# Gate blocks signalled column by column, squares between key blocks, and four value pages in the space of the prompt's keys

## The chip, the cores and the metric

One core of one Trainium2 chip runs the whole program in one launch. The metric is the device time of a launch in microseconds (us); less is better. TensorE (PE) multiplies matrices, VectorE (DVE), ScalarE (ACT) and GpSimd (POOL) work on tiles in on-chip memory (SBUF and the PSUM banks that PE writes), and SyncE (SP) issues the DMAs that bring weights and cache pages from HBM.

## What is computed

One inference step of one decoder layer, for a prompt of 512 tokens and a sample group of 8 single tokens (together T = 520 columns). The layer has a head group with stick-breaking attention, an S5 state-space group, cross-attention into 256 memory tokens and a convolutional feed-forward part. The change touches the stretch in which three things run side by side: the S5 gate, the memory keys, and the samples' attention over their cached value pages.

```python
# S5 group: y is 512 channels wide
y = jax.nn.gelu(y.reshape(bsz, t, SSM_WIDTH))
out = y * jax.nn.sigmoid(y @ w_glu + b_glu)            # the gate
...
mix = jnp.concatenate([_rmsnorm(o_sb, g_sb_out), _rmsnorm(o_ssm, g_ssm_out)], axis=-1)
x = x + mix @ w_out
...
m = _rmsnorm(mem, g_mem_kv)                            # memory keys and values
mk = (m @ w_mk).reshape(b, MEM_TOKENS, MEM_HEADS, MEM_HEAD_DIM)
...
k_past = cache_sb_k[l][page_table]                     # 8 samples x 2 pages of 128 tokens
v_past = cache_sb_v[l][page_table]
```

## The kernel before, in words

Everything is held channel-major: a tile has 128 channels on the partitions and tokens along the free axis. Matrices of weights come in 126 blocks of 512 KB, numbered in the order of use. Each block n takes the same path: SP loads it into `w_raw` slot n % 4 (`load_block`, L467 to L470, after the low parts of block n-4 are done); ACT copies its high part to `w_hi` slot n % 2 (`high`, L1238 to L1246, after PE has finished block n-2); POOL subtracts to get the low part `w_lo` in two halves (`low`, L581 to L587; DVE does it for a few early blocks); PE multiplies hi by hi, lo by hi and hi by lo (`three`, L620 to L627), in fp32r. Results of a block go to one of two PSUM slots (`slot(e)`, banks 0 and 1, or 2 and 3 of `pj`), and a slot is free again when DVE has read it: DVE adds to the semaphore `evacuated` with each read, PE adds to `block_done` with each finished block.

Every engine has its program written out by hand, and each runs it strictly in order; semaphores tie them together.

The stretch of the change, on PE (from L1012 on), is: `memory_keys(0)`, `memory_keys(1)`, `gate_columns(0)`, `memory_keys(2)`, `gate_columns(1)`, `memory_keys(3)`, `memory_keys(4)`, `decode_values(0)` and `(1)`, `memory_keys(5)`, the column sums of the squares of gated y (`feature_sums`, L683), `decode_values(2)`, `memory_keys(6)`, `decode_values(3)`, `memory_keys(7)`, and eight small matmuls (L1061), after which the memory values (blocks 26 to 33) begin. A memory-key block is 24 matmuls of 256 columns. A gate block (numbers 18 and 20) is two column blocks of 24 matmuls of 260 columns, one for each PSUM slot. The slots in order are e = 16, 17 (keys), 18, 19 (gate), 20 (keys), 21, 22 (gate), 23 to 27 (keys), so `memory_keys(2)` needs the slot of the first gate column block, and `memory_keys(3)` that of the third.

A gate column block is finished by ACT, which takes the sigmoid in PSUM (`gates`, L1442 to L1446), and by DVE, which multiplies it with y (`gate_y`, L1898 to L1901). In between on ACT stand the high parts of the weights and the squares of the gated y (`square`, L1252), which DVE adds up (`add_square`, L1584 for the first, L1587 for the others); the sum over channels and its inverse root (L1256, L1257) scale y. ACT's functions come in table sets: a change of set is a row of its own (ACT_TABLE_LOAD).

The samples' value pages: 16 pages of 256 KB, multiplied in four groups of four (`decode_values(g)`, L944 to L952, matmuls of 32 columns of weights; it adds 1 to `dav_pg`). Groups 0 and 2 use the buffer `vpg`, groups 1 and 3 `kpg`. SP's queue (L528 to L544) loads groups 0 and 1 early, then waits for `dav_pg` 1 before group 2 and for `dav_pg` 2 before group 3:

```python
            for n in range(22, 26):
                load_block(n)
            eng.wait_ge(dav_pg, 1)
            for m in range(8, 12):
                load_values(m)
            load_block(26)
            load_block(27)
            eng.wait_ge(dav_pg, 2)
            for m in range(12, 16):
                load_values(m)
            load_blocks(28, 40)
```

The prompt's keys `kT` (128 x 2080) are read last by the prompt's scores (`scores`, L885 to L903, which count `qk_done`) and by the store of the keys to HBM (counted by `kv_stored`). After the memory values the same space holds other things.

Of the kernel before, what the change touches and what calls it, by code (L numbers as in the profile page):

```python
# [19 lines left out]
ACT = mybir.ActivationFunctionType  # L20
# [7 lines left out]
T = TP + NS  # L28
# [3 lines left out]
SBW = 512  # L32
AT = SBW // P
HEADS = 8
# [22 lines left out]
MK_SLOT, GLU_SLOT = (16, 17, 20, 23, 24, 25, 26, 27), (18, 19, 21, 22)  # L57
# [44 lines left out]
def build(nc, xT, memT, wblk, cols_d, bc_d, dskip_d, consts_d, pages_d, kpool, vpool, kmem, vmem,  # L102
# [5 lines left out]
    def sem(name):  # L108
        return ctx.enter_context(nc.semaphore(name))
# [4 lines left out]
    with ctx:  # L114
# [28 lines left out]
        kT = sbuf(sbctx, "kT", [P, AT, T])  # L143
# [41 lines left out]
        yT = cube(near, 5632, AT, T)  # L185
# [6 lines left out]
        kpg = sbuf(midctx, "kpg", [P, 4, SBW])  # L192
        vpg = sbuf(midctx, "vpg", [P, 4, SBW])
# [13 lines left out]
        xctx.close()  # L207


        cache_tail = [t[:, :, :].rearrange("p a t -> p (a t)")[:, 4 * LANE * NS:4 * LANE * NS + D] for t in (qT, kT)]  # L210
        qz = [t[:, :, :].rearrange("p a t -> p (a t)")[:, 0:4 * LANE * NS].rearrange(
            "p (f c) -> p f c", f=4) for t in (qT, kT)]
# [29 lines left out]
        kv_stored = sem("kv_stored")  # L242
# [4 lines left out]
        block_done = sem("block_done")  # L247
        evacuated = sem("evacuated")
# [50 lines left out]
        qk_done = sem("qk_done")  # L299
# [25 lines left out]
        dav_pg = sem("dav_pg")  # L325
        dav_read = sem("dav_read")
        m_scaled = sem("m_scaled")
        m_hi_done = sem("m_hi_done")
        m_split = sem("m_split")
        sig_done = sem("sig_done")  # L330
        mix_scaled = sem("mix_scaled")
        s_done = sem("s_done")
# [29 lines left out]
        def col(name, i=0, n=1):  # L362
            return cols[:, COL[name] + i:COL[name] + i + n]
# [8 lines left out]
        def slot(e):  # L372
            return pj[:, 2 * (e % 2):2 * (e % 2) + 2, 0:HALF]
# [73 lines left out]
            return (kpg if n % 8 < 4 else vpg)[:, n % 4, :]  # L447

        def value_slot(m):
            return (vpg if m // 4 % 2 == 0 else kpg)[:, m % 4, :]  # L450

        o_bank = aux[:, 3, :]

# [10 lines left out]
        def _(sp_eng):  # L464
            eng = sp_eng
# [53 lines left out]
            def load_values(m):  # L519
                n = page_of(m)  # L520
                load_page(n, value_slot(m), vpool, vpg_loaded[m % 8])
# [6 lines left out]
            eng.wait_ge(dscore_pg, NS * PAGES)  # L528
            for m in range(8):
                load_values(m)  # L530
            for n in range(22, 26):
                load_block(n)
            eng.wait_ge(dav_pg, 1)
            for m in range(8, 12):
                load_values(m)
            load_block(26)
            load_block(27)
            eng.wait_ge(dav_pg, 2)
            for m in range(12, 16):
                load_values(m)  # L540
            load_blocks(28, 40)
            load_block(40)
            load_block(41)
# [76 lines left out]
        def _(pe):  # L620
# [400 lines left out]
            def gate_columns(g):  # L1021
                n = GLU_AT[g]
                wait_low(pe, n, 1)
                for j in range(2):
                    e = GLU_SLOT[2 * g + j]
                    pe.wait_ge(evacuated, e - 1)
                    for kt in range(AT):
                        if g + j == 0:
                            pe.wait_ge(y_split, kt + 1)
                        if (j, kt) == (0, 2):  # L1030
                            second_half(n)
                        hi, lo = (w[:, j * P:(j + 1) * P] for w in weight(n, kt, 2 * P))
                        ins = three([(slot(e)[:, a, :], hi, lo, halves(h_hi[:, AT + kt, :])[:, a, :],
                                      halves(h_lo[:, AT + kt, :])[:, a, :]) for a in range(2)],
                                    kt == 0, kt == AT - 1)
                ins.then_inc(block_done, 1)

            pe.wait_ge(a_exp, HEADS)
            memory_keys(0)
# [25 lines left out]
            for pair in range(4):  # L1065
                pe.wait_ge(evacuated, N_MV + (1, 2, 4, 6)[pair])
                for part in range(2):
                    n = N_MV + 2 * pair + part
# [168 lines left out]
        def _(act):  # L1237
            order = Order(act, act_order)  # L1238

            def high(n, i=0, step=4):  # L1240
                act.wait_ge(raw_loaded[n % 4], raw_count(n, i, step))
                if n == N_END - 2:
                    act.wait_ge(a_split, FT)
                elif n >= 2:
                    act.wait_ge(block_done, min(n, N_END - 2) - 1 + i * step)
                nc.scalar.activation(w_pair(n)[0], w_raw[:, n % 4, :], ACT.Copy).then_inc(hi_done, 1)  # L1246

            def square(src, width, j, i=0, per=0):

                if not (isinstance(j, int) and j == 0):  # L1250
                    act.wait_ge(acc_added, j + i * per)
                nc.scalar.activation(sq[:, 0:width], src, ACT.Square).then_inc(sq_ready, 1)  # L1252
# [186 lines left out]
                    high(18)  # L1439
            high(19)  # L1440

            def gates(first, last):  # L1442
                for m in range(first, last):
                    act.wait_ge(block_done, GLU_AT[m // 2] + 1)
                    nc.scalar.activation(slot(GLU_SLOT[m]), slot(GLU_SLOT[m]), ACT.Sigmoid,
                                         bias=col("b_glu", m)).then_inc(sig_done, 1)  # L1446

            high(20)
            gates(0, 2)
            high(21)  # L1450
            high(22)
            gates(2, 4)
            nc.scalar.preload_act_table_set("natural_log_exp_and_others")
            act.wait_ge(da_arg, 1)
            act.wait_ge(az_cleared, 1)
            nc.scalar.activation(az[:, :, :, :].rearrange("p t b w -> p (t b) w")[:, :, 8:16],
                                 dz[:, 2, :].rearrange("p (c h) -> p c h", h=HEADS), ACT.Exp).then_inc(da_ready, 1)
            high(23)
            act.wait_ge(evacuated, GLU_SLOT[3] + 1)
            square(yT[:, 0, :], T, 4)  # L1460
            square(yT[:, 1, :], T, 5)
            high(24)
            square(yT[:, 2, :], T, 6)
            square(yT[:, 3, :], T, 7)
            root(2, halves(rinv[:, :]), sums23, SBW)
            high(25)
            high(26)
# [74 lines left out]
            for i in range(FT // 2):  # L1542
                for c in range(2):
                    n = N_GU + 2 * c
# [29 lines left out]
        def _(dve):  # L1574
# [3 lines left out]
            def add_square(j, first, width=T, group=0, i=0, per=0):  # L1578

                dve.wait_ge(sq_ready, j + 1 + i * per)  # L1580
                if first:
                    if group:
                        dve.wait_ge(stats_done, group - 1)
                    nc.vector.tensor_copy(acc[:, 0:width], sq[:, 0:width]).then_inc(acc_added, 1)  # L1584
                else:
                    dve.wait_ge(acc_added, j + i * per)
                    tt(acc[:, 0:width], acc[:, 0:width], sq[:, 0:width], ALU.add).then_inc(acc_added, 1)  # L1587
# [300 lines left out]
            def read_keys(m):  # L1888
                dve.wait_ge(block_done, MK_AT[m] + 1)
                nc.vector.tensor_copy(mkT[:, m, :], slot(MK_SLOT[m])[:, 0, 0:MT]).then_inc(evacuated, 1)  # L1890
# [7 lines left out]
            def gate_y(first, last):  # L1898
                for m in range(first, last):
                    dve.wait_ge(sig_done, m + 1)  # L1900
                    tt(halves(yT[:, m, :]), slot(GLU_SLOT[m]), halves(yT[:, m, :]), ALU.mult).then_inc(evacuated, 1)  # L1901
# [57 lines left out]
            read_keys(1)  # L1959
            split_y(2, 4)  # L1960
            gate_y(0, 2)
            read_keys(2)
            gate_y(2, 4)
            read_keys(3)
            add_square(4, True, T, 2)
            add_square(5, False, T, 2)
            read_keys(4)
            add_square(6, False, T, 2)
            add_square(7, False, T, 2)
            read_keys(5)  # L1970
            inverted(2)
# [265 lines left out]
```

## Time and profile before

| | us |
|---|---|
| median of 3 runs | 928.23 |
| lowest and highest | 927.63, 929.48 |
| the profiled execution's own time | 930.51 |
| its span, first to last instruction | 928.7 |
| PE busy | 868.4 (94%) |
| DVE, ACT, POOL busy | 464.5, 334.1, 310.0 |

The profile is one execution. A row of the timeline gives the start, the length, the engine and line, output and inputs, a count, and in brackets how long the engine had been idle before it and what ended the wait. The granted clock (PEclk) is TensorE's, as a share of full speed. A matmul's length includes the time in which its result drains, so back-to-back matmuls overlap; what counts is the distance between starts.

### The profile page before, as it was taken

To read this page: it belongs to the slowest core of one execution; us is meant where nothing else is said; L and a number is where in the kernel's file an instruction comes from. 1 tells how busy PE (TensorE), PEld (TensorE's weight loads), DVE (VectorE), ACT (ScalarE), POOL (GpSimd) and SP (SyncE) were. 2 spreads that over 40 slices of the span, in tenths; PEclk is the share of its full clock that TensorE was granted. 3 is DMA by queue.
4 is the path that set the end of the run, shared out by engine and by line. 5 is a ranking of instruction groups with operands and counts; after the bars stand their busy time and mean duration, and the time that the engine had idled before them with its cause. 6 is when DMAs were issued, how large, how long until landed. Compare 5 with 4: busy or idle time off the path is not lost.

```text
span 928.7 us, 17749 instructions
## 1 busy us (share of the span) xinstructions
PE 868.4 (94%) x7422; PEld 811.5 (87%) x7422; DVE 464.5 (50%) x660; ACT 334.1 (36%) x491; POOL 310.0 (33%) x241
## 2 busy tenths in 40 slices
PE   5999897989977899899899999999999999999996
PEld 5989896867776889799559989999999999999996
DVE  5979777666513743511233465555566666201013
ACT  6553314443733432321332443333333333322231
POOL 4100002000144665344003534444444444445450
PEclk9999998987989999999999999999999999999999
DMA  8221203233325348521841223222232322232322
GB/s 308 70 70 46 70 24 148 88 92 91 93 89 182 109 137 326 201 81 57 331 167 48 92 73 107 92 91 92 91 92 91 92 91 92 92 112 94 97 69 92
DMA packets 30457, 103.97 MB, mean 112 GB/s; under 512 B 3866, under 2 KB 6170, under 8 KB 27954
## 3 DMA queue, kind: packets, MB, share of 16 engines
q1 hardware_dynamic: 30386, 102.91, 33.1%
q8 instruction: 58, 0.95, 0.4%
q14 instruction: 13, 0.11, 0.0%
HBM read 96.28 MB, written 6.71 MB: 111 GB/s over the span
## 4 chain that ended last, share of the span: by engine, by line
PE 70%; issue 11%; DVE 7%; POOL 5%; DMA 3%; ACT 3%; SPq 1%; POOLq 0%; DVEq 0%; ACTq 0%
PE pj L624 19%; PE pj L626 19%; PE pj L625 19%; POOL w_lo L586 4%; DMA w_raw<-in 3%; DVE h_lo L1591 2%; PE pj L1175 2%; PE aux L1106 2%; PE aux L702 1%; PE aux L714 1%; PE aux L765 1%; PE pj L898 1%; DMA caches<-in 1%; SPq L557 1%; PE pj L1137 1%
## 5 line engine op out<-in xcount | busy, mean ns | idle before, releaser
L586 POOL TENSOR_TENSOR w_lo<-w_raw,w_hi 128x512 fp32r<-128x512 f32 x224 | 301.0, 1365 | 563.2 <-ACT w_hi L1246 563.2
L624 PE MATMUL pj<-h_hi,w_hi 128*128 128x260 f32 x1312 | 376.7, 287 | 16.4 <-POOL w_lo L586 10.2
L626 PE MATMUL pj<-h_hi,w_lo 128*128 128x260 f32 x1312 | 372.2, 284 | 0.0
L625 PE MATMUL pj<-h_lo,w_hi 128*128 128x260 f32 x1312 | 371.4, 283 | 0.0
L624 PEld LDWEIGHTS pj<-h_hi,w_hi 128*128 128x128 f32 x1312 | 248.8, 190 | 19.6 <-POOL w_lo L586 12.5
L1246 ACT ACTIVATE w_hi<-w_raw 128x1024 fp32r<-128x1024 f32 x125 | 132.0, 1056 | 339.7 <-PE pj L626 305.1
L625 PEld LDWEIGHTS pj<-h_lo,w_hi 128*128 128x128 f32 x1312 | 248.5, 189 | 0.5
L626 PEld LDWEIGHTS pj<-h_hi,w_lo 128*128 128x128 f32 x1312 | 248.6, 189 | 0.0
L626 PE MATMUL pj<-a_hi,w_lo 128*128 128x260 f32 x336 | 95.1, 283 | 0.0
L624 PE MATMUL pj<-a_hi,w_hi 128*128 128x260 f32 x336 | 95.0, 283 | 0.0
L625 PE MATMUL pj<-a_lo,w_hi 128*128 128x260 f32 x336 | 95.0, 283 | 0.0
L626 PEld LDWEIGHTS pj<-a_hi,w_lo 128*128 128x128 f32 x336 | 63.4, 189 | 0.0
L624 PEld LDWEIGHTS pj<-a_hi,w_hi 128*128 128x128 f32 x336 | 63.3, 188 | 0.0
L625 PEld LDWEIGHTS pj<-a_lo,w_hi 128*128 128x128 f32 x336 | 63.3, 188 | 0.0
L2109 DVE TENSOR_TENSOR x<-pj,x 128x520 f32<-128x520 f32 x7 | 4.9, 699 | 88.4 <-PE pj L626 88.4
L2105 DVE TENSOR_TENSOR a_lo<-conv,a_hi 128x520 f32 x22 | 38.2, 1738 | 18.3 <-ACT a_hi L1557 18.3
L1587 DVE TENSOR_TENSOR acc<-acc,sq 128x520 f32<-128x520 f32 (+1 forms) x29 | 33.3, 1148 | 23.2 <-ACT sq L1252 23.2
L1554 ACT ACTIVATE conv<-conv 128x520 f32<-128x520 f32 x22 | 14.0, 638 | 74.6 <-DVE conv L2098 74.6
L2094 DVE SCALAR_TENSOR_TENSOR conv<-gate,cols,conv 128x512 f32<-128x512 f32 x22 | 39.6, 1798 | 0.0
L2010 DVE TENSOR_TENSOR x<-pj,x 128x520 f32<-128x520 f32 x16 | 11.2, 698 | 37.9 <-PE pj L626 37.9
L2090 DVE TENSOR_TENSOR gate<-pj,rinv 128x520 f32<-128x520 f32 x22 | 15.4, 699 | 27.3 <-PE pj L626 27.1
L1591 DVE SCALAR_TENSOR_TENSOR h_lo<-x,cols,h_hi 128x520 fp32r<-128x520 f32 x24 | 24.3, 1050 | 6.1 <-ACT h_hi L1265 6.0
(373 smaller groups left out, 1237.5 us busy)
## 6 DMA issues: line engine op xcount, KB each, us to landing
w_raw<-in SPq DMA_DIRECT2D x126, 512.0 KB, 3.5
caches<-in SPq DMA_DIRECT2D x14, 1024.0 KB, 12.4
kpg<-in SPq DMA_DIRECT2D x16, 256.0 KB, 3.0
vpg<-in SPq DMA_DIRECT2D x16, 256.0 KB, 3.0
x<-in SPq DMA_DIRECT2D x4, 520.0 KB, 7.8
out<-x SPq DMA_DIRECT2D x16, 130.0 KB, 1.9
out<-kT SPq DMA_DIRECT2D x1, 1040.0 KB
far<-in SPq DMA_DIRECT2D x1, 1024.0 KB, 4.9
```

The source lines that it names most:

```text
L586: nc.gpsimd.tensor_tensor(lo[:, part], w_raw[:, n % 4, part], hi[:, part].bitcast(F32), ALU.subtract).then_inc(lo_done, 1)
L624: pe.matmul(out, s_hi, m_hi_, start=first, stop=False)
L625: pe.matmul(out, s_hi, m_lo_, start=False, stop=False)
L626: ins = pe.matmul(out, s_lo, m_hi_, start=False, stop=last)
L1106: ins = pe.matmul(aux[:, 2 * (h % 2) + qt // 2, MT * (qt % 2):MT * (qt % 2 + 1)], qm[:, 2 * h + dd, P * qt:P * (qt + 1)], mkT[:, 2 * h + d ...
L1175: ins = pe.matmul(pj[:, 2 + dd, :], mv[:, kt, c:c + P], probT[:, kt, :], start=(kt == 0), stop=(kt == 1))
L1246: nc.scalar.activation(w_pair(n)[0], w_raw[:, n % 4, :], ACT.Copy).then_inc(hi_done, 1)
L1587: tt(acc[:, 0:width], acc[:, 0:width], sq[:, 0:width], ALU.add).then_inc(acc_added, 1)
L1591: stt(out=h_lo[:, kt, :], in0=x[:, kt, :], scalar=col(gain, kt), in1=h_hi[:, kt, :].bitcast(F32), op0=ALU.mult, op1=ALU.subtract).then_inc ...
L2090: tt(halves(gate[:, c, 2:T + 2]), slot(0), halves(rinv[:, :]), ALU.mult).then_inc(evacuated, 1)
L2094: order.done(stt(out=conv[:, c, 0:TP], in0=gate[:, c, 1:TP + 1], scalar=tap("conv_w1"), in1=conv[:, c, 0:TP], op0=ALU.mult, op1=ALU.add))
L2105: tt(a_lo[:, i * 2 + c, :], conv[:, c, :], a_hi[:, i * 2 + c, :].bitcast(F32), ALU.subtract).then_inc(a_split, 1)
```

## The change

Four things are changed. PE signals the first column block of each gate block by itself, on a new semaphore `gate_done`. ACT takes each sigmoid by itself, the first of each pair ahead of the next high part, with the table set loaded ahead, and takes three of the four squares earlier. DVE adds the squares earlier, between the key blocks' reads. Value pages 8 to 11 are loaded into `kT`, right after block 22; pages 12 to 15 go to `vpg` and wait for `dav_pg` 1 alone.

```diff
+        value_tail = kT[:, :, :].rearrange("p a t -> p (a t)")
...
         def value_slot(m):
-            return (vpg if m // 4 % 2 == 0 else kpg)[:, m % 4, :]
+            if m // 4 == 2:
+                return value_tail[:, SBW * (m % 4):SBW * (m % 4 + 1)]
+            return (kpg if m // 4 == 1 else vpg)[:, m % 4, :]
...
             for m in range(8):
                 load_values(m)
-            for n in range(22, 26):
+            load_block(22)
+            eng.wait_ge(kv_stored, 16 * 3)
+            eng.wait_ge(qk_done, HEADS)
+            for m in range(8, 12):
+                load_values(m)
+            for n in range(23, 26):
                 load_block(n)
             eng.wait_ge(dav_pg, 1)
-            for m in range(8, 12):
+            for m in range(12, 16):
                 load_values(m)
             load_block(26)
             load_block(27)
-            eng.wait_ge(dav_pg, 2)
-            for m in range(12, 16):
-                load_values(m)
             load_blocks(28, 40)
...
-                ins.then_inc(block_done, 1)
+                    ins.then_inc(*((gate_done, 1), (block_done, 1))[j])
...
-            def gates(first, last):
-                for m in range(first, last):
+            def open_gate(m):
+                if m % 2 == 0:
+                    act.wait_ge(gate_done, m // 2 + 1)
+                else:
                     act.wait_ge(block_done, GLU_AT[m // 2] + 1)
-                    nc.scalar.activation(slot(GLU_SLOT[m]), slot(GLU_SLOT[m]), ACT.Sigmoid,
-                                         bias=col("b_glu", m)).then_inc(sig_done, 1)
-
+                nc.scalar.activation(slot(GLU_SLOT[m]), slot(GLU_SLOT[m]), ACT.Sigmoid,
+                                     bias=col("b_glu", m)).then_inc(sig_done, 1)
+
+            nc.scalar.preload_act_table_set("sigmoid_and_others")
+            open_gate(0)
             high(20)
-            gates(0, 2)
+            open_gate(1)
+            act.wait_ge(evacuated, GLU_SLOT[0] + 1)
+            square(yT[:, 0, :], T, 4)
             high(21)
+            open_gate(2)
+            act.wait_ge(evacuated, GLU_SLOT[1] + 1)
+            square(yT[:, 1, :], T, 5)
             high(22)
-            gates(2, 4)
+            open_gate(3)
...
             high(23)
+            act.wait_ge(evacuated, GLU_SLOT[2] + 1)
+            square(yT[:, 2, :], T, 6)
             act.wait_ge(evacuated, GLU_SLOT[3] + 1)
-            square(yT[:, 0, :], T, 4)
-            square(yT[:, 1, :], T, 5)
+            square(yT[:, 3, :], T, 7)
             high(24)
-            square(yT[:, 2, :], T, 6)
-            square(yT[:, 3, :], T, 7)
             root(2, halves(rinv[:, :]), sums23, SBW)
...
             gate_y(0, 2)
+            add_square(4, True, T, 2)
             read_keys(2)
+            add_square(5, False, T, 2)
             gate_y(2, 4)
             read_keys(3)
-            add_square(4, True, T, 2)
-            add_square(5, False, T, 2)
+            add_square(6, False, T, 2)
             read_keys(4)
-            add_square(6, False, T, 2)
             add_square(7, False, T, 2)
```

ACT, from the high part of block 19 to the squares; before (w_hi is a high part, pj<-pj a sigmoid, sq a square, az the exponential that `decode_values(0)` waits for):

```order
L1246 ACTIVATE w_hi<-w_raw 128x1024 x2
L1445 ACT_TABLE_LOAD
L1445 ACTIVATE pj<-pj,cols 128x2x260 x2
L1246 ACTIVATE w_hi<-w_raw 128x1024 x2
L1445 ACTIVATE pj<-pj,cols 128x2x260 x2
L1453 ACT_TABLE_LOAD
L1456 ACTIVATE az<-dz 128x16x8
L1246 ACTIVATE w_hi<-w_raw 128x1024
L1252 ACTIVATE sq<-near 128x520 x2
L1246 ACTIVATE w_hi<-w_raw 128x1024
L1252 ACTIVATE sq<-near 128x520 x2
```

The same place after the change:

```order
L1252 ACTIVATE w_hi<-w_raw 128x1024
L1456 ACT_TABLE_LOAD
L1453 ACTIVATE pj<-pj,cols 128x2x260
L1252 ACTIVATE w_hi<-w_raw 128x1024
L1453 ACTIVATE pj<-pj,cols 128x2x260
L1258 ACTIVATE sq<-near 128x520
L1252 ACTIVATE w_hi<-w_raw 128x1024
L1453 ACTIVATE pj<-pj,cols 128x2x260
L1258 ACTIVATE sq<-near 128x520
L1252 ACTIVATE w_hi<-w_raw 128x1024
L1453 ACTIVATE pj<-pj,cols 128x2x260
L1468 ACT_TABLE_LOAD
```

The table load and the first sigmoid now stand ahead of block 20's high part, the second sigmoid behind it, and a square follows the second and the third sigmoid. There are as many table loads as before.

DVE, from the first gate product on, after the change (near<-pj,near is `gate_y`, keys<-pj the read of a key block, acc the sums of squares; before, the order was gate_y x2, keys, gate_y x2, keys, acc, acc, keys, acc x2, keys):

```order
L1915 TENSOR_TENSOR near<-pj,near 128x520 x2
L1598 COPY acc<-sq 128x520
L1904 COPY keys<-pj 128x256
L1601 TENSOR_TENSOR acc<-acc,sq 128x520
L1915 TENSOR_TENSOR near<-pj,near 128x520 x2
L1904 COPY keys<-pj 128x256
L1601 TENSOR_TENSOR acc<-acc,sq 128x520
L1904 COPY keys<-pj 128x256
L1601 TENSOR_TENSOR acc<-acc,sq 128x520
L1904 COPY keys<-pj 128x256
```

The second addition now stands ahead of the third gate product in DVE's queue.

## Rows read from the trace of the kernel before

**Rows 1.** The page: busy times, granted clock in 40 slices.

```profile
PE 868.4 (94%) x7422; PEld 811.5 (87%) x7422; DVE 464.5 (50%) x660; ACT 334.1 (36%) x491; POOL 310.0 (33%) x241
...
PEclk9999998987989999999999999999999999999999
```

**Rows 2.** Timeline of PE, 253 to 304 us: start, length, instruction, idle before it.

```profile
253.47 0.28 PE L624 MATMUL pj<-h_hi,w_hi 128*128 128x260 f32 x1
...
259.13 0.28 PE L626 MATMUL pj<-h_hi,w_lo 128*128 128x260 f32 x1
263.42 0.55 PE L624 MATMUL pj<-m_hi,w_hi 128*128 128x256 f32 x1 [4.01 <-DVE near L1901]
...
277.22 0.36 PE L624 MATMUL pj<-m_hi,w_hi 128*128 128x256 f32 x1 [2.59 <-POOL w_lo L586]
...
283.06 1.06 PE L950 MATMUL aux<-vpg,az 128*32 128x512 f32 x8
...
288.42 1.14 PE L683 MATMUL aux<-acc,consts 128*128 128x260 f32 x4 [0.40 <-DVE acc L1587]
292.00 1.34 PE L950 MATMUL aux<-vpg,az 128*32 128x512 f32 x8 [2.44 <-DMA vpg<-in]
...
299.58 1.07 PE L950 MATMUL aux<-kpg,az 128*32 128x512 f32 x8 [1.96 <-DMA kpg<-in]
...
303.52 0.96 PE L1061 MATMUL aux<-sel,az 128*128 128x8 f32 x8
```

**Rows 3.** Windows of this stretch: busy us (count) of PE, PEld, DVE, ACT, POOL, granted clock.

```profile
263.40:268.70 5.30, 5.28 (x25) 5.30 (x26) 0.48 (x1) 0.00 (x0) 0.00 (x0) 0.50 0.33 99
277.20:283.00 5.80, 5.78 (x48) 5.73 (x48) 1.90 (x3) 2.92 (x4) 2.64 (x3) 1.00 0.01 3
293.30:299.50 6.20, 4.32 (x27) 4.11 (x24) 1.76 (x3) 1.06 (x1) 2.05 (x3) 0.78 1.01 351
311.00:315.00 4.00, 2.89 (x11) 2.17 (x11) 3.16 (x5) 3.89 (x6) 3.16 (x3) 0.77 0.00 0
```

**Rows 4.** Timeline of ACT.

```profile
253.73 1.06 ACT L1246 ACTIVATE w_hi<-w_raw 128x1024 fp32r<-128x1024 f32 x1
259.50 1.06 ACT L1246 ACTIVATE w_hi<-w_raw 128x1024 fp32r<-128x1024 f32 x1 [4.71 <-PE pj L626]
260.57 1.28 ACT L1445 ACT_TABLE_LOAD   x1
261.87 1.25 ACT L1445 ACTIVATE pj<-pj,cols 128x520 f32<-128x520 f32 x2
```

**Rows 5.** Timelines of DVE and, in the last row, POOL.

```profile
262.57 1.30 DVE L1901 TENSOR_TENSOR near<-pj,near 128x520 f32<-128x520 f32 x2 [7.19 <-ACT pj L1445]
...
276.37 1.31 DVE L1901 TENSOR_TENSOR near<-pj,near 128x520 f32<-128x520 f32 x2 [7.03 <-ACT pj L1445]
...
283.81 1.00 DVE L1587 TENSOR_TENSOR acc<-acc,sq 128x520 f32<-128x520 f32 x1 [0.70 <-ACT sq L1252]
...
270.11 2.54 POOL L586 TENSOR_TENSOR w_lo<-w_raw,w_hi 128x512 fp32r<-128x512 f32 x2 [7.00 <-ACT w_hi L1246]
```

**Rows 6.** Timeline of SP's queue, columns as above.

```profile
254.24 18.77 SPq L470 DMA_DIRECT2D w_raw<-in  x4
284.89 4.01 SPq L514 DMA_DIRECT2D vpg<-in  x4
288.94 0.91 SPq L470 DMA_DIRECT2D w_raw<-in  x2
```

**Rows 7.** DMA issues at 254.24 (block 22), 288.56 (page 11), 288.94 (block 26): size, us to landing.

```profile
w_raw<-in SPq DMA_DIRECT2D x1, 512.0 KB, 3.6
...
vpg<-in SPq DMA_DIRECT2D x1, 256.0 KB, 3.3
...
w_raw<-in SPq DMA_DIRECT2D x1, 512.0 KB, 6.6
```

**Rows 8.** The scores' last matmuls (line 902).

```profile
L902 PE MATMUL pj<-never_r,consts_r x8: 415/416/475, 209.3 to 231.2; 128*128 128x128 f32 x8
```

More of the change, by code:

```diff
@@ L329, in build @@
         m_split = sem("m_split")
+        gate_done = sem("gate_done")
         sig_done = sem("sig_done")
```

## The prediction

> **What bounds the kernel now.** I read the page first: PE is busy 94% of the span, every other engine 50% or less, and the granted clock is at full speed in all but a few slices [rows 1]. So PE's stream of matmuls is the path, and a change can only win where PE stands still or runs at the lower of its two clock levels (1.2 instead of 2.4 GHz). Then I read PE's timeline through the stretch of the change, for the brackets: from the end of the first gate block (last matmul at 259.13, ended 259.41) to the eight small matmuls at 303.52 PE waits five times: 4.01 us for DVE's gate product, 2.59 us, put down to POOL's low part, 0.40 us for the sum of squares, 2.44 and 1.96 us for value pages [rows 2]. Third, the windows: the key block after the 4.01 us wait ran at a granted clock of 0.50 and took 5.3 us, where two such blocks took 5.8 us together at 1.00; the key block after the first wait for pages had 0.78 on average [rows 3]. Last, the timelines of ACT, DVE and SP, to see what each wait hangs on.
>
> The 4.01 us: when PE ends the gate block, ACT first makes block 20's high part (259.50, 1.06), loads a table set (1.28), and only then takes two sigmoids (1.25 together) [rows 4]; DVE's product begins at 262.57 [rows 5], and PE at 263.42. The 2.59 us is the same thing one gate block later, and its name misleads: the block that PE wants to start is 21, whose low part was whole at 272.65, while DVE's product that frees its PSUM slot ran from 276.37, 0.65 for the first, to 277.02 [rows 5], and PE began at 277.22. POOL's half of block 22 happened to end just then. So both gaps end with a product, which an earlier sigmoid moves. The waits for pages: SP issues pages 8 to 11 at 284.89, only after the first group is used, then blocks 26 and 27 at 288.94, then pages 12 to 15 [rows 6].
>
> **The change, part by part.** The new schedule is worked out from these durations: a column block of 24 matmuls 2.85 us (the distance of starts is 5.66/47 = 0.120 us [rows 2]), a key block 2.9 [rows 3], a high part 1.06 and a table load 1.28 [rows 4], one sigmoid or product 0.65 [rows 4, 5], half a low part 1.27 [rows 5], a square as long as a sigmoid, an addition 1.0 [rows 5].
>
> *Gate 0.* ACT ends high part 19 at 254.8 [rows 4], and loads the table until 256.1, while PE works. PE's first column block ends at 256.5; sigmoid to 257.2, product to 258.0. PE needs that slot at 259.25: the wait of 4.01 us is gone, with 1.2 us to spare. Late next is high part 20, which still starts at 259.50 (PE must have finished block 18): its first low half is there at 261.9, and the second product at 261.9. The key block ends at 262.1, so gate block 20 starts there, within 0.1 us of both.
>
> *Gate 1.* First column block ready 265.1, sigmoid to 265.8, then square and addition 5, which now stand ahead of the product on DVE: product done at 267.9. PE finishes the gate block at 267.8 and wants that slot then. I charge 0.2 us. High part 22 is at 268.1 to 269.1, the last sigmoid to 269.7, low part's first half at 270.5; the next key block wants both at 270.8. The 2.59 us are gone.
>
> *Table set and exponential* for the values: 269.7 to 271.3, wanted at 273.7. *High 23* then 271.3 to 272.3, its low part whole at 275.1, wanted at 275.6 and, its second half, 1.4 us later. *Squares 6 and 7* and their additions end at 275.6; their sum is wanted by PE at 278.4: 0.40 us gone. The instructions are the same in number on all engines, so none of this adds work; the two semaphore signals ride on matmuls that exist.
>
> *Pages.* SP's queue: block 22 at 254.24 as before, then four page loads (4.0 us for four [rows 6]) and block 23 some 0.8 us later than now. Its high part is wanted at 271.3, so this costs nothing. The waits ahead of them are met: the last scores ran at 231.2 [rows 8], and the program issues the store of the keys before it loads block 20. Pages 8 to 11 land by 262, wanted at 279.5: 2.44 us gone. Pages 12 to 15 wait for group 0: in the trace the first issue comes 1.83 us after its first matmul [rows 2, 6], so 275.5, the last 3.7 us later (288.56 against 284.89) at 279.2, landed 3.3 us after [rows 7] at 282.5; wanted at 283.4: 1.96 us gone, but by 0.9 us only.
>
> *Block 26,* which feeds the memory values, is now queued behind pages 12 to 15: issued at 279.5. Such a block lands after 3.6 us alone and took 6.6 us where other loads crowded it [rows 7]; so 283.1 to 286.1. Its high part is wanted at 283.5 and its low part when the values start (288.3): at the early end nothing is lost, at the late end 2.6 us of delay eat about 1.0 us of PE. Three blocks (26, 27, 28) go out together and no pages behind them; I take 284.5, cost 0. The Trainium skill ("DMA: Bandwidth & Descriptors", section on queues, rings and completion order) says that each DMA engine consumes its queue's descriptors in ring order. By that rule alone block 26 would not suffer from 27 and 28 behind it, and the cost would be 0 even at the late end; the 6.6 us in the row speak against relying on it.
>
> *Clock.* Without the 4.01 us wait the key block after it runs in 2.9 instead of 5.3 us: 2.4. The one after the pages: 4.32 us busy [rows 3] against 2.9: 1.4; group 2 of the values 1.34 against 1.06 [rows 2]: 0.3. The Trainium skill ("TensorE: Matmul & The Clock Gate", part on the clock gate) gives the distance of matmuls as columns / 1.2 GHz at the low level and columns / 2.4 GHz + 2.5 ns at the high one, which is 213 and 109 ns for 256 columns. The low one agrees with the trace (5.3 us for 25), the high one does not (120 ns); by the page the first term would be an estimate of 2.5, not 2.4.
>
> *Sum.* Waits 4.01 + 2.59 + 0.40 + 2.44 + 1.96 = 11.4. Each wait that goes also gives back 0.16, since a matmul then starts 0.12 after its forerunner instead of after its 0.28 [rows 2]: 0.8. Clock 2.4 + 1.4 + 0.3 = 4.1. Less 0.2 for gate 1: **16.1 us**. As a check, the schedule puts the end of the last key block at 287.3, where it is 303.52 now: 16.2. I take 16.0. Behind that point PE, ACT and DVE run off each other's semaphores, and SP's loads too, so nothing there is tied to an absolute time and the gain should pass to the end whole. The profiled execution took 930.5 with a span of 928.7; the span should become 912.7. The median of the runs is 928.23; it should become **912.2**.
>
> **The rivals.**
>
> *A, a leftover.* One of the tight places does not close: pages 12 to 15 (0.9 us of room), DVE's second addition ahead of the third product, or block 26. Bounds: 1.96 for the pages, as now; for DVE up to 1.0, if the addition starts that late; 1.0 for block 26. If the wait is followed by the low clock, 1.4 to 2.4 more. Together up to 5 us: the gain is 11 to 14.5, the time 913.7 to 917.2. For it speaks that the margins are under 1 us and that each is worked out from durations of about 0.05 us accuracy; against it, that each alone costs little.
>
> *B, clock lost elsewhere.* The clock also fell to 0.77 at 311 to 315, where PE had waited only about 1 us by then [rows 3]. The value groups (matmuls with 32 columns of weights) and the sum of squares are now packed between 273.7 and 283.4, and light work there may bring the lower level: 2.4 us for one key block. That is within A's range. The other way, if that drop at 311 vanishes in the new phase, 1.4 us more is won (15 matmuls at 0.09): 910.8.
>
> *C, given back later.* The transfers around the cross-attention caches could be what ends a later stage. If half the gain went there: 920. Against it: those loads are issued by SP after semaphores of the same chain, so they move with it.
>
> *D, slower.* If TensorE ran the whole packed stretch at the lower level, each of its 192 matmuls (48 of the gate, 144 of keys) would cost 0.213 - 0.120 = 0.093 us more, 17.9 us, against 16.1 won: 930.1. It decides from about 173 slow matmuls on; the trace has at most some 40 in this stretch, all after waits [rows 3].
>
> *E, the change does nothing:* PE might have been held at 259 by something else than the product. The row names DVE, and low part 19 was long done; 928.
>
> **How the numbers follow.** Within 0.2% of before (1.9 us, about what a measurement of this kernel can tell from no change) counts as the same. Forecast (gain 14.5 to 17.7) 0.74; A and B together 0.18; C 0.04; E 0.02; D 0.02. The range goes from 910.4 (all margins hold and the later drop vanishes as well) to 917.0 (most of A), with some 0.9 of the chance inside. Faster 0.96, same 0.02, slower 0.02.
>
> **What would show it.** In the new profile: no bracket over 0.5 us on PE's matmuls between 253 and 290; granted clock 1.00 there; the sigmoid at about 256.6 and again at 265.2; the eight small matmuls at 287.3; pages 12 to 15 issued from 275.5; the rest of the rows shifted by 16. I am wrong if the first key block after the gate still starts later than 259.5, if group 3 of the values waits for its pages, or if the end moves by less than the small matmuls do.

## The result, and the profile after

The changed kernel took 913.48 us, median of 4 runs (911.29 to 918.72), against 928.86 for the kernel before in the same comparison: ratio 0.9839, 95% interval [0.9802, 0.9875]. Twice more, in jobs of its own, it gave 0.9827 [0.9804, 0.985] and 0.981 [0.979, 0.983]. So it is 15 to 17 us faster; 912.2 was forecast.

The profiled execution of the first job was its slowest, 918.72 us with a span of 916.9. That is 11.8 us below the profile before and not 16, so the first question was where the other 4 are. The stretch of the change answers for itself. First PE's timeline in the changed kernel, from the first gate block to the eight small matmuls (start, length, instruction; a bracket would give the idle time before it):

```profile
257.76 0.28 PE L630 MATMUL pj<-h_hi,w_hi 128*128 128x260 f32 x1
...
263.54 0.28 PE L630 MATMUL pj<-m_hi,w_hi 128*128 128x256 f32 x1
...
272.19 0.36 PE L630 MATMUL pj<-m_hi,w_hi 128*128 128x256 f32 x1
...
278.04 1.06 PE L956 MATMUL aux<-vpg,az 128*32 128x512 f32 x8
...
282.83 1.04 PE L689 MATMUL aux<-acc,consts 128*128 128x260 f32 x4
283.80 1.06 PE L956 MATMUL aux<-kT,az 128*32 128x512 f32 x8
...
287.82 1.06 PE L956 MATMUL aux<-vpg,az 128*32 128x512 f32 x8
...
291.76 0.95 PE L1067 MATMUL aux<-sel,az 128*128 128x8 f32 x8
```

There is no bracket: all five waits of [rows 2] are gone. From 257.76 to 291.76 are 34.00 us, where it was 303.52 - 253.47 = 50.05: **16.05 us less** (forecast: 16.1 by the sum). The stretch as one window, in the kernel before and then in the changed one (busy us and count of PE, PEld, DVE, ACT, POOL; then clock, DMA share, GB/s):

```profile
253.40:303.60 50.20, 38.80 (x280) 34.10 (x279) 13.97 (x21) 17.47 (x22) 22.73 (x17) 0.90 0.40 129
```

```profile
257.70:291.80 34.10, 34.10 (x280) 30.28 (x279) 13.76 (x21) 17.26 (x22) 21.93 (x17) 1.00 0.57 182
```

The same 280 matmuls take 38.8 us of 50.2 at a mean clock of 0.90 before, and 34.1 of 34.1 at 1.00 now. So of the 16 us, 11.4 are idle time and 4.7 busy time. The starts of the matmuls split the 4.7. The key block behind the 4.01 us wait took 5.26 us from its first start to the next block's (263.42 to 268.68) and takes 2.84 now (263.54 to 266.38). The 24 matmuls behind the first wait for pages took 4.07 us from first to last start and take 2.83, and the value group ahead of them 1.27 and now 0.99: together 3.9 us at the lower clock level. The other 0.7 is overlap: at each of the five waits the distance of starts was 0.07 to 0.17 us longer than the bracket and the usual distance together, because the matmul that waited did not overlap the one before it. What differs from the forecast is the begin: 257.76 instead of 253.47, 4.3 us late, in a part of the program that the change does not touch.

ACT in the changed kernel, the rows that answer to [rows 4]:

```profile
258.01 1.06 ACT L1252 ACTIVATE w_hi<-w_raw 128x1024 fp32r<-128x1024 f32 x1
259.09 1.28 ACT L1456 ACT_TABLE_LOAD   x1
260.86 0.67 ACT L1453 ACTIVATE pj<-pj,cols 128x520 f32<-128x520 f32 x1 [0.48 <-PE pj L632]
263.80 1.06 ACT L1252 ACTIVATE w_hi<-w_raw 128x1024 fp32r<-128x1024 f32 x1 [2.28 <-PE pj L632]
264.77 0.65 ACT L1453 ACTIVATE pj<-pj,cols 128x520 f32<-128x520 f32 x1
...
269.48 0.67 ACT L1453 ACTIVATE pj<-pj,cols 128x520 f32<-128x520 f32 x1 [1.79 <-PE pj L632]
...
288.63 1.06 ACT L1252 ACTIVATE w_hi<-w_raw 128x1024 fp32r<-128x1024 f32 x1 [2.51 <-DMA w_raw<-in]
```

The table load now runs while PE works; the first sigmoid waits 0.48 us for PE and starts 2.9 us ahead of the high part that used to come first; the third (269.48) comes before PE has ended the gate block. The last row is block 26's high part: it waited 2.51 us for its load, the tight place of the forecast, but PE did not have to wait for it.

DVE, the answer to [rows 5], and SP's queue, the answer to [rows 6]:

```profile
261.56 0.70 DVE L1915 TENSOR_TENSOR near<-pj,near 128x520 f32<-128x520 f32 x1 [1.89 <-ACT pj L1453]
265.45 0.70 DVE L1915 TENSOR_TENSOR near<-pj,near 128x520 f32<-128x520 f32 x1 [3.19 <-ACT pj L1453]
266.07 0.46 DVE L1598 COPY acc<-sq 128x520 f32<-128x520 f32 x1
...
270.74 0.70 DVE L1601 TENSOR_TENSOR acc<-acc,sq 128x520 f32<-128x520 f32 x1 [3.74 <-ACT sq L1258]
271.36 0.69 DVE L1915 TENSOR_TENSOR near<-pj,near 128x520 f32<-128x520 f32 x1
```

```profile
259.70 4.39 SPq L518 DMA_DIRECT2D kT<-in  x4
264.13 6.54 SPq L474 DMA_DIRECT2D w_raw<-in  x3
279.87 3.66 SPq L518 DMA_DIRECT2D vpg<-in  x4
283.57 0.91 SPq L474 DMA_DIRECT2D w_raw<-in  x2
```

The first addition (266.07) comes between product and key block at no cost. The second, at 270.74, does stand ahead of the third product at 271.36, and that product ends at 272.05, just when PE wants it (PE's last gate matmul starts at 272.05, the next block at 272.19). Pages 8 to 11 go out at 259.70, blocks 23 to 25 behind them. Pages 12 to 15 go out from 279.87, 1.83 us after the first value group's first matmul (278.04), as before.

### The profile page after: what moved, and what is told of

Read it like the earlier page. It is cut to its first block, busy times and chain, and to the rows that moved or that the text cites. A ratio compares the mean times of both kernels' runs of the same rounds, so it can differ in the third digit from the quotient of the medians.

```text
span 916.9 us, 17753 instructions
## 1 busy us (share of the span) xinstructions
PE 867.8 (95%) x7422; PEld 811.3 (88%) x7422; DVE 464.3 (51%) x660; ACT 333.7 (36%) x491; POOL 309.6 (34%) x241
## 4 chain that ended last, share of the span: by engine, by line
PE 72%; issue 9%; DVE 7%; POOL 5%; DMA 3%; ACT 3%; SPq 1%; POOLq 0%; DVEq 0%; ACTq 0%
PE pj L630 19%; PE pj L632 19%; PE pj L631 19%; POOL w_lo L592 5%; DMA w_raw<-in 3%; DVE h_lo L1605 2%; PE pj L1181 2%; PE aux L1112 2%; PE aux L708 1%; PE pj L904 1%; PE aux L918 1%; PE aux L720 1%; PE aux L771 1%; DMA caches<-in 1%; SPq L563 1%
```

## The experiments

Each kernel was profiled once and timed in 5 rounds beside the kernel before. "Stretch" is the time from the first gate matmul to the eight small matmuls: 50.05 us before, 34.00 in the changed kernel.

### 1. The changed kernel again

> The changed kernel once more. Its first profile showed the stretch from the first gate block to the eight small matmuls shortened by 16.05 us, but begun 4.3 us later than before (257.8 instead of 253.5), with more half-speed clock ahead of it. Theory: the late begin is chance in TensorE's clock, so here the stretch again lasts 34.0 us, while its begin falls anywhere from 252 to 259; median of the runs 911 to 914. Rival: the change itself delays the begin; then it is at 257 to 258 again and the median is 914 to 917.

No edit. Measured: 912.73 us (911.53 to 914.13), stretch 254.56 to 288.73, 34.17 us, no wait. The begin is at 254.56, not at 257.8. The expectation held: the change is not what delayed the begin. The third profile of this kernel begins at 254.32 (below). The late begin is taken up again in the last section.

### 2. Pages alone, and gates alone

> Kernel before with only the page part (pages 8 to 11 in the keys' space, 12 to 15 behind the first group). Theory (the parts add up): the waits of 2.44 and 1.96 us go, with 0.16 each and 1.7 us of clock: the stretch is 6.1 to 6.4 us shorter, time 6 below before; the gate waits of 4.0 and 2.6 us stay. Rival (the page waits are only what the gate leaves over, and nothing is gained alone): under 2 us.

Against the kernel before:

```diff
+            if m // 4 == 2:
+                return value_tail[:, SBW * (m % 4):SBW * (m % 4 + 1)]
...
+            load_block(22)
+            eng.wait_ge(kv_stored, 16 * 3)
+            eng.wait_ge(qk_done, HEADS)
+            for m in range(8, 12):
+                load_values(m)
...
             eng.wait_ge(dav_pg, 1)
-            for m in range(8, 12):
+            for m in range(12, 16):
                 load_values(m)
...
-            eng.wait_ge(dav_pg, 2)
-            for m in range(12, 16):
-                load_values(m)
```

> Changed kernel without the page part (pages loaded as before, gate and squares as changed). Theory: up to the first value group it runs like the changed kernel, 9.4 us earlier than before; the pages of groups 2 and 3 then come the same time after group 0 as before, so PE waits about 3.0 us for group 2 and 2 to 3.5 us for group 3: gain 9.4 us in all, time 919. Rival (the page waits shrink once the gate waits are gone, so the page part is not needed): gain 14 or more.

Against the changed kernel:

```diff
-            if m // 4 == 2:
-                return value_tail[:, SBW * (m % 4):SBW * (m % 4 + 1)]
...
-            eng.wait_ge(kv_stored, 16 * 3)
-            eng.wait_ge(qk_done, HEADS)
-            for m in range(8, 12):
-                load_values(m)
...
             eng.wait_ge(dav_pg, 1)
-            for m in range(12, 16):
+            for m in range(8, 12):
                 load_values(m)
...
+            eng.wait_ge(dav_pg, 2)
+            for m in range(12, 16):
+                load_values(m)
```

PE's timeline of the kernel with the pages alone, its waits in the stretch, and the last value group, which has none:

```profile
264.65 0.55 PE L629 MATMUL pj<-m_hi,w_hi 128*128 128x256 f32 x1 [4.01 <-DVE near L1906]
...
278.84 0.36 PE L629 MATMUL pj<-m_hi,w_hi 128*128 128x256 f32 x1 [2.59 <-POOL w_lo L591]
...
290.03 1.15 PE L688 MATMUL aux<-acc,consts 128*128 128x260 f32 x4 [0.38 <-DVE acc L1592]
291.10 1.06 PE L955 MATMUL aux<-kT,az 128*32 128x512 f32 x8
...
295.14 1.07 PE L955 MATMUL aux<-vpg,az 128*32 128x512 f32 x8
```

The page waits are gone and the gate waits stand as before, 4.01 and 2.59 us. The stretch is 299.08 - 254.67 = 44.41 us, 5.64 less (expected 6.1 to 6.4: the lower clock behind the 4.01 us wait lasted 0.4 us into the next block here, clock 0.93 over 269.9 to 276.2). Time 924.23 us, ratio 0.9935 [0.9911, 0.9959].

And with the gates alone:

```profile
282.81 1.04 PE L684 MATMUL aux<-acc,consts 128*128 128x260 f32 x4
286.94 1.25 PE L951 MATMUL aux<-vpg,az 128*32 128x512 f32 x8 [3.09 <-DMA vpg<-in]
...
293.09 1.07 PE L951 MATMUL aux<-kpg,az 128*32 128x512 f32 x8 [0.54 <-DMA kpg<-in]
```

No gate wait is left; the page waits are 3.09 and 0.54 us. The stretch is 297.03 - 257.74 = 39.29 us, 10.76 less. The first wait came as expected. For the second, 2 to 3.5 us were expected: the pages were issued as long after group 0 as before (285.57 - 278.01 = 7.56 us; 290.63 - 283.06 = 7.57), but landed in 4.1 to 5.4 us instead of the 5.5 to 6.8 of the kernel before. Why they came earlier stays open: the two weight blocks ahead of them and the next one behind them were issued at the same distances in both kernels (1.7 us before the first page, 0.4 us after the last). **The two parts add up:** 5.64 + 10.76 = 16.40, against 16.05 for both. Neither rival holds, though the second wait for pages did shrink by itself, from 1.96 to 0.54 us. In whole runs the sum is short: 921.41 us, ratio 0.9915 [0.9892, 0.9937], is 7.9 below the 929.3 before, where the stretch says 10.8. This profile too begins late, at 257.74; whether the unprofiled runs did is not recorded, so the 2.9 us stay open.

### 3. Without the early signal

> Changed kernel, but each sigmoid waits for the whole gate block, as before; order of the instructions as changed. Theory (the early signal does about a third): PE waits 1.7 us after the first gate block and 3.0 us after the second, 4.9 us more with what overlaps, time about 918, and 2.4 us more if the clock falls behind the second wait. Rival 1 (the order alone does it, the signal is not needed): within 1 us of the changed kernel. Rival 2 (all of the gate's gain hangs on the signal): 7 us or more lost.

```diff
-                if m % 2 == 0:
-                    act.wait_ge(gate_done, m // 2 + 1)
-                else:
-                    act.wait_ge(block_done, GLU_AT[m // 2] + 1)
+                act.wait_ge(block_done, GLU_AT[m // 2] + 1)
```

```profile
262.63 0.36 PE L630 MATMUL pj<-m_hi,w_hi 128*128 128x256 f32 x1 [1.59 <-DVE near L1912]
...
274.20 0.36 PE L630 MATMUL pj<-m_hi,w_hi 128*128 128x256 f32 x1 [2.75 <-DVE near L1912]
```

```profile
274.20:281.50 7.30, 7.30 (x48) 7.24 (x48) 2.10 (x3) 3.20 (x5) 3.51 (x4) 0.77 0.01 2
```

The waits are 1.59 and 2.75 us (1.7 and 3.0 expected), the stretch is 295.30 - 255.11 = 40.19 us, 6.2 more than in the changed kernel: 4.3 of waits, and the 48 matmuls behind the second at a clock of 0.77, 7.3 us instead of 5.8. Time 919.88, ratio 0.9892 [0.9866, 0.9918]. The first rival falls. The second (7 us or more) falls by the stretch; in whole runs the loss is 7.2 us (919.88 against 912.73), which can't decide it. Taking the signal away thus costs 6.2 of the 10.8 us of the gate part, more than half and not about a third. This isn't the signal's price alone. The third sigmoid ended at 272.16 (271.49 and 0.67), but the moved square and its addition stand ahead of the product in this kernel, and the product began at 273.36: some 1.2 of the 2.75 us are theirs. The signal alone in the kernel before was not run.

The 2.75 us wait also settles the name in the bracket of [rows 2]. The product here ended at 274.05 and PE started at 274.20, while POOL's half of block 22, which began at 273.74 and took about 1.26, ended only at 275.0: PE did not wait for it. In the kernel before the two ended 0.11 us apart (277.02 and 277.13) and the bracket took the later one.

### 4. Squares where they were

> Changed kernel with the squares of gated y and their additions where they stood before (ACT: two behind high part 23, two behind high part 24). Theory (moving the squares is worth little): PE's sum of squares (1.04 us, no wait in the changed kernel) waits 0.4 to 1.0 us again, and the third gate product comes up to 0.5 us earlier without effect; stretch 34.4 to 35.0 us instead of 34.0, time within 1 us of the changed kernel. Rival (the squares between the key blocks carry a good part of the gain): stretch 37 us or more.

```diff
+            act.wait_ge(evacuated, GLU_SLOT[3] + 1)
+            square(yT[:, 0, :], T, 4)
+            square(yT[:, 1, :], T, 5)
             high(24)
+            square(yT[:, 2, :], T, 6)
+            square(yT[:, 3, :], T, 7)
```

(and the four earlier squares and DVE's additions moved back with them)

```profile
278.82 1.14 PE L689 MATMUL aux<-acc,consts 128*128 128x260 f32 x4 [0.68 <-DVE acc L1598]
```

The wait is 0.68 us, the third gate product is not waited for, the stretch is 288.04 - 253.03 = 35.01 us: 0.8 to 1.0 us more than with the squares moved (34.00 to 34.17 in three profiles). That is the theory's top end. Time 914.9 (911.35 to 918.8): too wide to show 1 us.

### 5. Without the explicit table load

> Changed kernel without the explicit early load of the sigmoid's table set, so that the load comes behind the wait for the first column block. Theory (1.2 us of room): sigmoid 1.3 us later, the product that frees the slot just when PE wants it; PE's wait at the first key block 0 to 0.3 us, stretch 34.0 to 34.3. Rival (the load ahead of time is what closes the first gap): wait of 1.3 us or more, stretch 35.4 or more. Second rival: the load is placed ahead of the wait anyway, so nothing moves.

```diff
-            nc.scalar.preload_act_table_set("sigmoid_and_others")
             open_gate(0)
```

```profile
255.60 1.28 ACT L1453 ACT_TABLE_LOAD   x1
257.35 0.67 ACT L1453 ACTIVATE pj<-pj,cols 128x520 f32<-128x520 f32 x1 [0.47 <-PE pj L632]
```

The load still runs right behind high part 19, ahead of the wait, and starts 1.75 us before its sigmoid: the second rival holds, nothing moved (stretch 288.27 - 254.25 = 34.02; 912.72 us). The 1.2 us of room that I had worked out was therefore not tested.

### 6. Blocks 26 and 27 ahead of the last pages

> Changed kernel with blocks 26 and 27 loaded ahead of value pages 12 to 15 instead of behind them. Theory (pages land 1.3 us before PE wants them in the changed kernel, and take 5.5 us instead of 3.0 behind two blocks): PE waits 1.5 to 2.5 us for the last value group, stretch 35.7 to 36.7, and 1.4 us more if the clock falls behind the wait. Rival (what counts is only the buffer; the order of the loads is indifferent): no wait, stretch 34.0.

```diff
             eng.wait_ge(dav_pg, 1)
+            load_block(26)
+            load_block(27)
             for m in range(12, 16):
                 load_values(m)
-            load_block(26)
-            load_block(27)
```

```profile
277.58 3.64 SPq L518 DMA_DIRECT2D vpg<-in  x4
```

```profile
284.63 1.06 PE L956 MATMUL aux<-vpg,az 128*32 128x512 f32 x8
```

No wait: the theory falls. Stretch 288.75 - 254.57 = 34.18 us, 913.97 us. The last page was issued at 280.9 and landed 3.3 us later, at 284.2; PE wanted the four at 284.63. The 5.5 us that I had taken for "behind two blocks" came from [rows 7]'s neighbourhood in the kernel before, where two blocks stood ahead of the pages and two more followed; here SP issued a page every 1.1 us behind the two blocks. Which of the two made the difference was not tested. The order of these loads is worth nothing as measured, but it leaves 0.4 us of room.

This kernel also shows something about block 26. Issued at 275.96 with nothing ahead of it, and with block 27 and the pages behind it (from 276.5 on), it landed after 3.5 us, as fast as a block alone; block 27, with block 26 ahead, took 4.5.

### 7. Further: the next stage

Three kernels in one job: the changed kernel as base, and two that try the waits behind the stretch.

> The changed kernel a third time, as the base of the two that follow. Theory of the clock's chance: stretch 34.0 to 34.2 us, median 911 to 914.

> Changed kernel with block 28's high part on ACT between the second and third square of the other head group, instead of behind all four and two more copies. In the changed kernel POOL idles some 4 us there, then makes low parts without a pause for 25 us while PE waits 0.3 to 1.0 us for them five times. Theory (those waits begin with the late high part 28): POOL starts 3 us earlier, PE's waits for low parts of 1.03, 0.66, 0.35 us shrink, the sum of squares comes 1 us later; 1 to 2 us gained against the changed kernel. Rival (the later sum of squares, which sets the scale that the projection's inputs wait for, takes it back): within 0.5 us, or slower.

```diff
             for a in range(AT):
                 square(osb[:, a, :], T, 8 + a)
+                if a == 1:
+                    high(N_MV + 2)
```

> As the one before, and PE's sum of squares behind the first half of the second pair of memory-value blocks. Theory: the wait of 0.9 us for the sum is covered too, so 2 to 3 us are gained against the changed kernel. Rival: the scale comes 3 us later, the four products of 1.25 us each that wait for it end later, and the output projection waits for its inputs: nothing gained, or 1 to 2 us lost.

```diff
-                if pair == 0:
+                    if (pair, part) == (1, 0):
                         pe.wait_ge(acc_added, 12)
                         pe.wait_ge(dav_read, 1)
                         feature_sums(0, (HALF, HALF)).then_inc(stats_done, 1)
```

The base: 913.81 us (911.38 to 915.32), stretch 288.34 - 254.32 = 34.02. With the high part earlier 914.84, with the sum moved as well 912.99: no difference that these runs can tell. (The kernel with the sum moved has the earlier high part too.) PE's waits in the base, then in the kernel with the earlier high part:

```profile
296.05 1.14 PE L689 MATMUL aux<-acc,consts 128*128 128x260 f32 x4 [0.89 <-DVE acc L1601]
...
298.22 0.36 PE L637 MATMUL pj<-w_hi,m_hi 128*128 128x256 f32 x1 [1.03 <-POOL w_lo L592]
...
299.83 0.38 PE L637 MATMUL pj<-w_hi,m_hi 128*128 128x256 f32 x1 [0.67 <-POOL w_lo L592]
```

```profile
297.15 1.94 PE L689 MATMUL aux<-acc,consts 128*128 128x260 f32 x4 [2.03 <-DVE acc L1604]
```

In the kernel with the sum moved as well, the sum has no bracket, but behind it stand:

```profile
301.43 0.38 PE L637 MATMUL pj<-w_hi,m_hi 128*128 128x256 f32 x1 [0.63 <-POOL w_lo L592]
...
304.88 0.35 PE L637 MATMUL pj<-w_hi,m_hi 128*128 128x256 f32 x1 [1.07 <-POOL w_lo L592]
```

POOL's low parts in the kernel with the earlier high part:

```profile
293.56 2.98 POOL L592 TENSOR_TENSOR w_lo<-w_raw,w_hi 128x512 fp32r<-128x512 f32 x2 [1.25 <-ACT w_hi L1252]
298.16 2.97 POOL L592 TENSOR_TENSOR w_lo<-w_raw,w_hi 128x512 fp32r<-128x512 f32 x2 [1.62 <-ACT w_hi L1252]
303.95 6.18 POOL L592 TENSOR_TENSOR w_lo<-w_raw,w_hi 128x512 fp32r<-128x512 f32 x4 [2.82 <-ACT w_hi L1252]
```

POOL does start 3 us earlier (293.56; 296.81 in the base) and the waits of 1.03 and 0.67 us vanish, but the sum of squares is waited for 2.03 instead of 0.89 us, and behind it POOL waits 2.82 us for a high part. From the small matmuls to the output projection it is 31.78 us, 31.69 in the base and 31.91 in the other kernel. The rivals hold as to the time: nothing is gained. Covering the sum's wait doesn't help either, since waits for low parts come in its place; so the sum alone does not tie this stage. From 303 us on POOL works 3.16 of 3.4 us a block in the base, so the round of high part, low part and matmuls is the likely limit; no run here tested that.

## Why the prediction was right

*The reading* that the path is PE's stream, and that each gap ends with a product, a sum of squares or a page, held at all five places: no wait is left in the timeline, and the partial kernels show each wait returning when its cause returns.

*Gate 0 and 1.* The waits of 4.01 and 2.59 us went. Of the 0.2 us charged for DVE's addition ahead of the third product about 0.1 was needed: PE's first two starts there come 0.14 and 0.20 us after the one before instead of 0.12. For the second wait it mattered not to take the name in the bracket at its word: with POOL as the cause one would have looked for an earlier low part, and the product was it (experiment 3).

*Pages.* Both waits went. The room for pages 12 to 15 was 0.9 us by the sum and 0.6 by the trace: the last, issued at 283.18, landed after 4.0 us instead of 3.3, and was wanted at 287.82. Block 26 I had put at 5.0 us from issue to landing; issued at 283.57, it took 5.0, and cost PE nothing. It came after the page issued ahead of it (287.2). The Trainium skill says that each DMA engine takes its queue's descriptors in ring order ("DMA: Bandwidth & Descriptors", section on queues, rings and completion order); it does not promise that loads also finish in that order, but here they did. The prediction held the 6.6 us of [rows 7] against leaning on that rule. The runs point the other way: the 6.6 us block had four pages ahead of it, while experiment 6's block 26, with loads only behind it, took 3.5. So what stood ahead made the block late, and what came behind did not, as that rule has it. This is one pair of loads, not a series.

*Clock.* Forecast 4.1 us for the half-speed matmuls, and 0.8 for the overlap that comes back with each wait; together 4.9. Measured: busy time 38.80 to 34.10, 4.7, of which 3.9 is clock (2.4, 1.2 and 0.3, where 2.4, 1.4 and 0.3 were forecast). The 1.4 was too large because the 4.32 us busy of [rows 3] run to the end of the last matmul, while the 2.9 set against them is a distance of starts.

*Sum.* 16.1 by the sum, 16.05 measured in the stretch. The schedule gave 33.8 us from the first gate matmul to the small ones (253.47 to 287.3); it is 34.00.

*Given back later* (rival C) did not happen: from the small matmuls to the end it is 625.2 us before and 625.1 after, and between 621.0 and 625.2 in the ten other profiles. The time of 912.2 is within 1.6 us of all three medians. That it is so close is partly luck: the runs of the changed kernel spread from 911.3 to 918.7, which the forecast had not reckoned with. The baseline's own runs went from 925.1 to 933.8 over the jobs, while the three I started from spanned 1.9; so the 0.2% given as what a measurement can tell was too fine for so few runs.

*Rival B* was half right: the packed stretch did not bring the low clock, and the drop that had stood at 311 came in one profile and not in another: 0.81 at 299 to 303 in the first, 1.00 at the same place (296 to 300) in the repeat. Nothing in the forecast said which it would be.

## What to carry to other kernels

Where two engines hand a PSUM slot back and forth, signal each slot by itself and put the work that frees a slot ahead of the work that feeds a later block: here taking away one semaphore increment, placed one column block earlier, cost 6.2 of the 16 us. A buffer that has been read for the last time (here the keys, read 23 us before) can serve as one more page buffer: 5.6 us here by itself, while swapping the order of two loads in the changed kernel was worth nothing. And cost a wait on PE by what follows it: 3.9 of the 16 us were matmuls at half clock.

## What the runs showed of the hardware

TensorE's clock is not the same from run to run outside the stretch, and the times go with it: in the first job's four runs the mean granted clock was 0.970 for 918.72 us, 0.974 for 915.13, 0.978 for 911.29 and 0.976 for 911.83.

The late begin goes with it too. Over 180 to 240 us the granted clock is 0.80 in the first profile and in the one with the gates alone, the two that begin at 257.8 and 257.7, and 0.83 to 0.86 in the ten others. The first and the third profile of the changed kernel are 0.3 us apart in the prompt's scores at 187 us (187.37 and 187.08), and 2.7 us apart at the two matmuls of line 982 (207.11 and 204.44).

After the wait behind the first normalisation (PE busy 4.63 of 7 us) the first profile has:

```profile
380.00:388.00 8.00, 8.00 (x52) 7.61 (x52) 0.70 (x1) 2.19 (x3) 2.53 (x2) 0.79 0.01 2
```

and the repeat of the same kernel, at nearly the same place:

```profile
377.00:385.00 8.00, 8.00 (x68) 7.97 (x67) 1.40 (x2) 3.25 (x4) 3.22 (x3) 1.00 0.21 63
```

52 matmuls against 68 in 8 us (65 if the second window begins as long after the wait as the first). The part behind the small matmuls lasted 625.1 us in one and 621.0 in the other, and the begin of the stretch lay between 253.0 and 257.8 over all twelve profiles. The same wait does not always bring the same clock: behind the waits of 0.90 and 1.03 us for the sum and the low part, the first profile has 0.81, the third, with 0.89 and 1.03, has 1.00. For the longer waits of the stretch: behind 2.59 us the next two blocks ran at 1.00 [rows 3], behind 2.75 us at 0.77, behind 3.09 us (gates alone) at 0.66 from 288.0 to 292.6, behind 4.01 us the next block at 0.50 both times. So one profile can be 4 us off in either direction, while the stretch of the changed kernel came out within 0.2 us in its three profiles (34.00, 34.17, 34.02); the stretch is what to compare.
